# Key/value and query units of a sparse attention computed from split weights and inputs, with the gates' products ahead of the queries

## What is computed

```python
def second_block(...):
    for layer in range(DEPTH):
        h = h + 0.5 * _swiglu(_rmsnorm(h, ffn1_norm[layer]), ...)
        u = _rmsnorm(h, mix_norm[layer])
        h = h + (_s5_mixer(u, ...) if layer == 0 else _nsa_mixer(u, kv, w_qg, q_norm, w_o, rel_bias))
        h = h + 0.5 * _swiglu(_rmsnorm(h, ffn2_norm[layer]), ...)
        if layer == 0:
            kv = _shared_kv(h, kv_norm, w_kv, ...)

def _shared_kv(h, kv_norm, w_kv, ...):
    kv = (_rmsnorm(h, kv_norm) @ w_kv)           # 1024 -> 1536
    ...

def _nsa_mixer(u, kv, w_qg, q_norm, w_o, rel_bias):
    qg = u @ w_qg                                # 1024 -> 1024 queries and 48 gates
    q = _rmsnorm(qg[..., :N_HEADS * HEAD_DIM], q_norm)
    gates = sigmoid(qg[..., N_HEADS * HEAD_DIM:])
    ...
```

## Time and profile before

| what | value |
|---|---|
| median of 3 runs | 3513.84 us (3512.36 to 3518.11) |
| the profiled execution, its own time | 3517.05 us |
| its span, first to last instruction | 3514.9 us |
| TensorE busy | 3240.9 us, 92% |
| VectorE busy | 2340.7 us, 67% |
| ScalarE busy | 1572.0 us, 45% |
| granted clock, mean over the span | 0.949 |

### The profile page before, as it was taken

How to read it: one execution, slowest core, us unless ns; L and a number is a source line. 1 busy time by engine, 2 the same in 40 slices (tenths; PEclk the granted TensorE clock), 3 DMA queues, 4 the chain that set the end, 5 groups by cost and what they waited for, 6 DMA issues and landing times. The chain is left out here.

```text
span 3514.9 us, 51411 instructions
## 1 busy us (share of the span) xinstructions
PE 3240.9 (92%) x20778; PEld 2907.5 (83%) x20778; DVE 2340.7 (67%) x2644; ACT 1572.0 (45%) x1529; POOL 107.5 (3%) x102
## 2 busy tenths in 40 slices
PE   6998899999899699999999999898469998998999
PEld 6988799999787588788788888798249988996799
DVE  7976368846761488888788888497964432446444
ACT  3443244434340277677677777333014312334433
POOL 0003000000220000000000000000000000000000
PEclk9999999989999799999999999999689996999999
DMA  7630278734203099999899999254024532551253
GB/s 304 260 144 1 72 276 309 270 120 174 96 1 120 14 363 367 340 368 368 333 362 363 370 369 367 98 188 157 0 96 151 184 133 61 189 179 49 72 180 131
DMA packets 130378, 703.21 MB, mean 200 GB/s; under 512 B 11008, under 2 KB 16144, under 8 KB 74384
## 3 DMA queue, kind: packets, MB, share of 16 engines
q1 hardware_dynamic: 118384, 650.30, 50.4%
q0 software_dynamic: 6368, 47.19, 3.4%
q10 hardware_dynamic: 5440, 3.17, 0.3%
HBM read 698.50 MB, written 1.07 MB: 199 GB/s over the span
## 5 line engine op out<-in xcount | busy, mean ns | idle before, releaser
L1143 DVE TENSOR_TENSOR ring_low<-ring,parts 128x2048 fp32r<-128x2048 f32 x570 | 1298.1, 2287 | 393.1 <-ACT parts L2025 365.4
L454 PE MATMUL banks<-parts 128*128 128x256 f32 (+1 forms) x3712 | 1170.1, 315 | 43.6 <-DVE tail_parts L1143 25.3
L455 PE MATMUL banks<-tail_parts,parts 128*128 128x256 f32 x3744 | 1062.0, 284 | 0.0
L2025 ACT ACTIVATE parts<-ring 128x2048 fp32r<-128x2048 f32 x234 | 448.4, 1917 | 847.1 <-PE banks L456 726.1
L456 PE MATMUL banks<-parts,ring_low 128*128 128x256 f32 x2816 | 797.8, 283 | 0.0
L454 PEld LDWEIGHTS banks<-parts 128*128 128x128 f32 x3712 | 707.9, 191 | 85.6 <-issue 47.1
L2092 ACT ACTIVATE parts<-ring 128x2048 fp32r<-128x2048 f32 x336 | 644.5, 1919 | 237.5 <-DMA ring<-in_wall 219.8
L455 PEld LDWEIGHTS banks<-tail_parts,parts 128*128 128x128 f32 x3744 | 712.1, 190 | 1.9 <-issue 1.9
L456 PEld LDWEIGHTS banks<-parts,ring_low 128*128 128x128 f32 x2816 | 537.3, 191 | 0.0
L455 PE MATMUL banks<-ring_low,parts 128*128 128x512 f32 x896 | 355.0, 396 | 0.0
L456 PE MATMUL banks<-parts,tail_parts 128*128 128x512 f32 x896 | 352.5, 393 | 0.0
(11 more groups left out here) (396 smaller groups left out, 3584.6 us busy)
## 6 DMA issues: line engine op xcount, KB each, us to landing
ring<-in_wall SPq DMA_DIRECT2D x616, 1024.0 KB, 6.4
big<-in_wall POOLq DMA_DIRECT2D x40, 1024.0 KB, 5.4
big<-in_w_k POOLq DMA_DIRECT2D x1, 2048.0 KB, 7.9
big<-in_w_v POOLq DMA_DIRECT2D x1, 2048.0 KB, 13.7
big<-bias_table ACTq DMA_DIRECT2D x2, 1024.0 KB, 6.9
constants<-in_con SPq DMA_DIRECT2D x1, 1377.5 KB, 7.3
x<-in_x SPq DMA_DIRECT2D x1, 1024.0 KB, 9.3
big<-big ACTq DMA_DIRECT2D x16, 64.0 KB, 2.0
```

The lines of the kernel that those rows point to most:

```text
L454: pe.matmul(o, high, in_high, start=start, stop=False, **kw)
L455: pe.matmul(o, high, in_low, start=False, stop=False, **kw)
L1143: return ve.tensor_tensor(out, a, b, op)
L2025: act(parts(w_high(room, n), UNIT), ring[n % RING][:, :], ACT.Copy).then_inc(sem("w_high"), 1)
```

## The change

The six key/value units and the four query units go through `cols_split`. The norms ahead of them make high and low parts of `H`; `w_hi` and `w_low` split the units, in the rooms `ROOM_KVU` (new) and `ROOM_KV`. On VectorE the low part of key/value unit u + 2 stands ahead of the copy of unit u; in the query loop the low part of unit u + 2 stands behind the copy of u and ahead of the scaling of u - 1, and on ScalarE its high part behind the square of u. The gates' products stand ahead of the query units, chunk by chunk, and `h_low`, which overwrites `H`, waits for them (`gates_part`, `gate_logits`).

```diff
@@ -242,16 +242,18 @@
         ROOM_KV = (3072, 5120, 7168)
+        ROOM_KVU = (16896, 18944, 20992)
         NORM_BANK = (7, 7, 0, 7, 7, 7, 0, 7, 0, None, 0, 7)
...
         splits = blocks_before = 0
-        for name, count in (("w_in0", 0), ("ffn", BLK1), ("w_in1", 0), ("ffn1_0", BLK2), ("ffn2_0", BLK2), ("ffn1_1", BLK2),
-                            ("ffn2_1", BLK2)):
+        for name, units, count in (("w_in0", PROJECTIONS, 0), ("ffn", 3 * BLK1, BLK1), ("w_in1", PROJECTIONS, 0),
+                                   ("ffn1_0", 3 * BLK2, BLK2), ("ffn2_0", 3 * BLK2, BLK2), ("kv", 6, 0), ("ffn1_1", 3 * BLK2, BLK2),
+                                   ("q", 4, 0), ("ffn2_1", 3 * BLK2, BLK2)):
             SPLITS[name], SPLIT_BLOCKS[name] = splits, blocks_before
-            splits += 3 * count if count else PROJECTIONS
+            splits += units
             blocks_before += count
@@ -980,7 +982,8 @@
             for u in range(6):
-                cols_unit(UN["kv"] + u, lambda t: half(u, t), normed=None if u else 8)
+                pe.wait_ge(sem("w_low"), SPLITS["kv"] + u + 1)
+                cols_split(UN["kv"] + u, lambda t: half(u, t), ROOM_KVU, None if u else "kv")
             stage_end(pe, "pe")
@@ -1036,15 +1039,20 @@
+            for k in range(KT):
+                pe.wait_ge(*at("normed", k + 1, 10))
+                for n in range(NT):
+                    mm = pe.matmul(bank[4][:, n * 48:n * 48 + 48], H[:, k * TOK + n * P:k * TOK + (n + 1) * P],
+                                   par("w_gate", 48, k * 48), start=(k == 0 and n == 0), stop=(k == KT - 1), skip_group_check=True)
+                if k == KT - 1:
+                    mm.then_inc(event("gate_logits")[0], 1)
+                elif k % 2:
+                    mm.then_inc(sem("gates_part"), 1)
             for u in range(4):
-                cols_unit(UN["q"] + u, lambda t: half(u, t), normed=None if u else 10)
+                pe.wait_ge(sem("w_low"), SPLITS["q"] + u + 1)
+                cols_split(UN["q"] + u, lambda t: half(u, t), ROOM_KV, None if u else "q")
                 if u:
                     q_sum(u - 1)
-            for n in range(NT):
-                for k in range(KT):
-                    mm = pe.matmul(bank[4][:, n * 48:n * 48 + 48], H[:, k * TOK + n * P:k * TOK + (n + 1) * P],
-                                   par("w_gate", 48, k * 48), start=(k == 0), stop=(k == KT - 1))
-            mm.then_inc(event("gate_logits")[0], 1)
@@ -1150,6 +1158,10 @@
                         ve.wait_ge(*at("ba", c + 1, i // 2))
+                    if split == "q" and c < 3:
+                        ve.wait_ge(sem("gates_part"), c + 1)
+                    elif split == "q":
+                        ve.wait_ge(*event("gate_logits"))
                     tt(parts(HB + c * 512, 512), H[:, c * 512:(c + 1) * 512], parts(h_high(room) + c * 512, 512).bitcast(F32),
@@ -1853,9 +1865,11 @@
             ffn2("ffn2_0", 0)
-            norm_v(norms, ("kv_norm", 0), False)
+            norm_v(norms, ("kv_norm", 0), False, split="kv", room=ROOM_KVU)
             norms += 1
             for u in range(6):
+                if u + 2 < 6:
+                    w_low(UN["kv"] + u + 2, SPLITS["kv"] + u + 3, ROOM_KVU)
                 ve.wait_ge(sem("unit_done"), UN["kv"] + u + 1)
@@ -1920,7 +1934,7 @@
             ffn2("ffn1_1", 1)
-            norm_v(norms, ("mix_norm", 8), False)
+            norm_v(norms, ("mix_norm", 8), False, split="q", room=ROOM_KV)
             norms += 1
@@ -1965,6 +1979,8 @@
                 ve.tensor_copy(big(QB + u * 512, 512), bank[u][:, :]).then_inc(sem("q_out"), 1)
+                if u + 2 < 4:
+                    w_low(UN["q"] + u + 2, SPLITS["q"] + u + 3, ROOM_KV)
                 if u:
@@ -2316,8 +2332,10 @@
             ffn2("ffn2_0")
-            norm_s(norms)
+            norm_s(norms, split="kv", room=ROOM_KVU)
             norms += 1
+            for u in range(2, 6):
+                w_hi(UN["kv"] + u, ROOM_KVU)
             stage_end(se, "se")
@@ -2351,7 +2369,7 @@
             ffn2("ffn1_1")
-            norm_s(norms)
+            norm_s(norms, split="q", room=ROOM_KV)
             norms += 1
@@ -2387,6 +2405,8 @@
                 act(big(PT + u * 512, 512), big(QB + u * 512, 512), ACT.Square).then_inc(sem("q_sq"), 1)
+                if u + 2 < 4:
+                    w_hi(UN["q"] + u + 2, ROOM_KV)
                 if u:
```

## The result

The kernel with the change takes **3525.75 us** (median of 15 runs, 3516.38 to 3530.32) against 3515.15 us before (15 runs, 3512.20 to 3520.39) on the same chip: a ratio of 1.0029 with a 95% interval of 1.0023 to 1.0036. It is slower by 10.6 us, where +3.1 was forecast, and lies above the range.

The account below looks back on a forecast made before the run. TensorE was taken to bound the key/value stretch, VectorE the query stretch after unit 3. Terms -3.2 + 6.1 + 0.2 = +3.1 us on 3513.84 gave 3516.9 us, range 3511.5 to 3521.5.

Parts of the forecast that it names:

- Unit pace: Key/value and query stretches: a split unit takes 5.72 us on TensorE, 1.23 us less than the plain 6.95.
- Start of the key/value units: Key/value stretch: first split product 2.42 us after the first scaling, slower start, faster units after it; net -3.2 us.
- The bound for a start without a fall of the clock: Key/value start: if the clock never fell, unit 0 done near 9.7 us after the first scaling, gain 4.0 us.
- Gates ahead: Query start: gates now on the path, clock falling in their middle; copy of unit 0 13.9 us after first scaling, +6.1 us.
- the warm case: Query start: clock holds through the gates, costing +3.1 us there; total -0.7 to +0.1, about 3513.5 us; chance 0.27.
- From copy 0 to the bias: Query stretch, unit 0's copy to attention's first bias: VectorE is the bound, faster units bring nothing; +0.2 us.
- the second rival (TensorE bound): Query stretch: attention has slack behind the first bias, only TensorE's end counts; -3.4 us there, 3506.4 us total; chance 0.05.
- Everything behind that bias is one chain and moves with it: Attention onward, after the first bias: one chain of waits that shifts with the bias, no further cost added.
- the clock stays low into attention (slower): Attention's first group: half clock still there at 3226 costs an estimated 4.5 us more; +7.6, 3521.4 us; chance 0.13.
- Eight us of dense work lie between: Ahead of attention's first group: eight us of dense work, argued against the half clock reaching 3226.

Follow-up runs that it names:

- the kernel with the norms filled: Changed kernel with gates behind the queries, query scaling ahead of the low half, plus three idle TensorE products behind five norms' sums: 3508.05 us, ratio 0.9976.
- typical profile: Profiled execution of the changed kernel run once more without any edit, standing for most executions: 3530.14 us.
- first profile: Profiled execution of the changed kernel as first measured, no further edit, fastest of its fifteen: 3516.38 us.
- two additions: Kernel before with two useless VectorE additions of 512 columns ahead of attention's first bias: 3525.19 us, ratio 1.0028; with four such additions 3518.33 us, ratio 1.0004.
- second measurement: Changed kernel timed and profiled again, unedited, against the kernel before: 3529.25 us over 8 runs, ratio 1.0035.

## Why the prediction was wrong

**Unit pace: right.** 5.72 us in both stretches.

**Start of the key/value units: right.** -3.0 us against -3.2, with 2.42 to the first product. The bound for a start without a fall of the clock, unit 0 near 9.7, was met by the kernel with the norms filled (38.36 - 5 x 5.72 = 9.76).

**Gates ahead: right.** Copy 0 at S + 13.8 to S + 14.3 against 13.9, with the fall in the middle of the gates where it was put (full clock in the first half, 0.50 from S + 4.6 in the typical profile and from S + 2.7 in the first). In the first profile the halves fit too (first split product at S + 6.3, copy 7.4 us later; forecast 6.3 and 7.6). In the typical one they are 5.8 and 8.5: two misses nearly cancel there, which is luck. The choice against the warm case held for a reason that the forecast had only half: even with no pause ahead the clock falls, after the narrow products instead of among them.

**From copy 0 to the bias: right.** 28.4 us; forecast 28.8 (5.72 + 23.1), before 28.7. VectorE is the bound, the units' pace brings nothing, and the second rival (TensorE bound) falls.

**"Everything behind that bias is one chain and moves with it": the step that failed.** It moves, but not at unchanged durations. The chain runs over TensorE from the second group on, and whether TensorE is at 2.4 or 1.2 GHz there depends on when it comes, not only on what is in it. The change shifts the bias against the clock's steps to 0.56 us behind one, and attention costs 7.25 us more. That the moment is the cause is shown, not argued: two additions put the kernel before to 0.43 us and gave it the same 7.27 us, and twice as many took them away. What in this moment the chip answers to, the length of the wait or its place, is not shown.

The **rival "the clock stays low into attention (slower)"** is the one that came about, and its chance of 0.13 was too small. Its place was right: half clock on the chain behind 3226. Its condition, the first half clock reaching that place, was not met: at 3231.84, when TensorE comes back on the chain in the typical execution, the clock is full, and it falls 1.6 us later. Its price for the first group was estimated at 4.5 us and measured at 14.38 - 8.90 = 5.5; 1.8 us more came from the group behind, which it left out. Its way was wrong: the low clock of the query chain does end in time, at about 3223.2 in the typical execution, and a **second** fall follows ten us later. "Eight us of dense work lie between" was the argument against it. That work is products of 128 and 256 columns and ends in a wait of 1.86 us, which could be read from the timeline of before, and rows 7 and 8 already showed the clock falling in narrow products behind a pause of 2.07 us.

**Left out besides:** the +1.49 us between the stretches. In the feed-forward stage behind the compressed keys the clock is at half when it begins. Before:
```profile
2964.00:2969.70 5.70, 3.41 (x15) 3.40 (x16) 5.61 (x13) 2.52 (x4) 0.00 (x0) 0.50 0.00 0
2969.90:2975.00 5.10, 5.10 (x45) 5.10 (x44) 2.02 (x1) 0.99 (x1) 0.00 (x0) 1.00 0.01 3
```
After, typical:
```profile
2962.00:2970.50 8.50, 6.10 (x28) 6.09 (x29) 7.93 (x14) 2.52 (x4) 0.00 (x0) 0.50 0.00 0
```
The stage's first scaling is at 2963.88 and 2961.98; the clock rises 5.9 and 8.6 us behind it, each time on a step. So a stage that starts earlier need not get its full clock earlier, and half of what the key/value stretch gained went there. In the first profile of after the rise comes 5.3 us behind the scaling, and nothing is lost.

The range failed with the same step: its high end of 3521.5 was this rival's typical value, with nothing for its own scatter.

## What to carry to other kernels

When a stage is moved by a few microseconds, ask of every wait of TensorE behind it whether the clock can fall there, and price that case with the whole stretch up to the next rise, not with the moved microseconds; two parts can bring it together that do not bring it alone. Test it by a short useless delay on the path, in the kernel before too: if more work takes less time, the moment decides and not the work. In this kernel the split paid only where TensorE did not rest while the operands were split, and the narrow products cost most ahead of dense ones that are on the path. Look also where an idle product lands: one that waits for the same semaphore as the work behind it fills no wait.

## What the runs showed of the hardware

- The changes of the granted clock lie on a regular raster of each execution. A stage that starts at half clock gets the full clock on a step of it, and so the program may be carried along: seven of eight executions of after in the second measurement (3526.89 to 3533.81 us), and all nine of before with two additions (3522.14 to 3528.79 us), have times that fit the same price, though the start of the key/value stretch scatters by 8 us over the profiles. That the stages ahead lock the attention to the raster is only argued; what is shown is that a delay of 1.2 us of the first bias brings the fall in the kernel before and one of 2.4 us does not.
- A wait of 2.08 to 2.17 us among products of 128 and 256 columns at full clock was followed by some 17 us at 1.2 GHz in which TensorE is fully busy (three profiles). Waits of 1.37 to 1.97 us in the same place, at other distances from the steps, cost nothing, and neither did one of 2.12 us with 1.98 us of 512-column products behind it, but for these products' own time.
- The Trainium skill's TensorE: Matmul & The Clock Gate, Part 1, has activity release the throttled state. The rows agree that dense work brings the full clock back, and show beyond it that dense work after narrow work can still run into a fall: 18 records of split products at 0.50, with TensorE busy 5.44 of the 6.10 us ahead of them.
